# Last projections of a two-block network: turning activations inside the next projection, norm factor applied at eviction

## The reference, cut to what matters

```python
y_hg = o_hg @ w_hg_out                                  # 1024 -> 2048
y_at = swa_sinks(qa, ka, va, sinks) @ w_at_out          # 1024 -> 2048
mixed = sigmoid(g_hg) * y_hg + sigmoid(g_at) * y_at
x = x + mixed @ w_out                                   # 2048 -> 2048
h2 = rmsnorm(x, norm_ffn)       # x * rsqrt(mean(x*x) + eps) * norm_ffn
x = x + square(relu(h2 @ w_up)) @ w_down                # 2048 -> 8192 -> 2048
```

## Time and profile before

| | us |
|---|---|
| median of 3 runs | 2844.6 |
| lowest and highest of them | 2839.79, 2845.03 |
| the profiled execution | 2837.94 |
| its span in the trace | 2836.0 |
| PE busy | 2599.0 (92%) |
| DVE busy | 1644.5 (58%) |
| ACT busy | 1307.8 (46%) |
| POOL busy | 346.7 (12%) |

### The profile page before, as it was taken

How to read it: one execution, slowest core, us unless ns; L and a number is a source line. 1 busy time by engine, 2 the same in 40 slices (tenths; PEclk the granted TensorE clock), 3 DMA queues, 4 the chain that set the end, 5 groups by cost and what they waited for, 6 DMA issues and landing times.

```text
span 2836.0 us, 35750 instructions
## 1 busy us (share of the span) xinstructions
PE 2599.0 (92%) x12310; PEld 2150.9 (76%) x12310; DVE 1644.5 (58%) x2435; ACT 1307.8 (46%) x1761; POOL 346.7 (12%) x242
## 2 busy tenths in 40 slices
PE   3579999999996899989789999999889999999999
PEld 2468877888885788768678778778668888888887
DVE  6877887777767644445575555544344444544543
ACT  2234444444434444434446666654444444444443
POOL 2200122111012000000000000005101111111111
PEclk9689999999998899999799999999989999999999
DMA  8878767878874634434345555535346655556553
GB/s 294 287 271 286 272 230 256 278 267 281 274 245 170 201 104 119 125 103 167 121 151 154 160 168 155 164 133 194 133 136 193 190 192 182 190 193 189 182 192 134
DMA packets 354931, 548.56 MB, mean 193 GB/s; under 512 B 31788, under 2 KB 117136, under 8 KB 354448
## 3 DMA queue, kind: packets, MB, share of 16 engines
q1 hardware_dynamic: 353152, 541.37, 57.6%
q10 hardware_dynamic: 1680, 5.91, 0.5%
HBM read 545.13 MB, written 2.10 MB: 193 GB/s over the span
## 4 chain that ended last, share of the span: by engine, by line
PE 62%; DVE 3%; ACT 2%; issue 1%; POOL 0%; ACTq 0%; DVEq 0%; POOLq 0%
PE ps L1256 18%; PE ps L1257 18%; PE ps L1258 18%; PE ps L1316 1%; PE ps L1253 1%; PE ps L1254 1%; PE ps L1255 1%; PE ps L1465 1%; PE ps L1466 1%; PE ps L1332 0%; DVE a_lo L750 0%; DVE tf L770 0%; ACT hi L370 0%; ACT a_hi L469 0%; DVE stage L1033 0%
## 5 line engine op out<-in xcount | busy, mean ns | idle before, releaser
L668 DVE TENSOR_TENSOR lo<-raw,hi 128x1024 fp32r<-128x1024 f32 x838 | 1046.5, 1262 | 869.2 <-ACT hi L370 867.8
L370 ACT ACTIVATE hi<-raw 128x1024 fp32r<-128x1024 f32 x838 | 879.0, 1058 | 834.2 <-PE ps L1258 804.6
L1256 PE MATMUL ps<-hi,a_hi 128*128 128x512 f32 (+2 forms) x2464 | 983.0, 399 | 43.8 <-DVE lo L668 29.4
L1257 PE MATMUL ps<-lo,a_hi 128*128 128x512 f32 (+2 forms) x2464 | 965.2, 392 | 0.0
L1258 PE MATMUL ps<-hi,a_lo 128*128 128x512 f32 (+2 forms) x2464 | 964.9, 392 | 0.0
L1256 PEld LDWEIGHTS ps<-hi,a_hi 128*128 128x128 f32 x2464 | 469.4, 190 | 153.3 <-issue 39.6
L1258 PEld LDWEIGHTS ps<-hi,a_lo 128*128 128x128 f32 x2464 | 468.9, 190 | 98.9
L1257 PEld LDWEIGHTS ps<-lo,a_hi 128*128 128x128 f32 x2464 | 469.7, 191 | 91.1
L1256 PE MATMUL ps<-hi,b_hi 128*128 128x512 f32 (+1 forms) x896 | 336.1, 375 | 1.4 <-DVE b_lo L746 1.4
L1257 PE MATMUL ps<-lo,b_hi 128*128 128x512 f32 (+1 forms) x896 | 334.9, 374 | 0.0
L1258 PE MATMUL ps<-hi,b_lo 128*128 128x512 f32 (+1 forms) x896 | 334.9, 374 | 0.0
(11 more groups left out here) (235 smaller groups left out, 1719.6 us busy)
## 6 DMA issues: line engine op xcount, KB each, us to landing
raw<-in_ada_w SPq DMA_DIRECT2D x96, 1024.0 KB
raw<-in_sgu_w_in SPq DMA_DIRECT2D x96, 1024.0 KB
raw<-in_w_up SPq DMA_DIRECT2D x64, 1024.0 KB
raw<-in_w_down SPq DMA_DIRECT2D x64, 1024.0 KB
raw<-in_w_in SPq DMA_DIRECT2D x42, 1024.0 KB
raw<-in_sgu_w_out SPq DMA_DIRECT2D x32, 1024.0 KB
raw<-in_w_in SPq DMA_DIRECT2D x128, 256.0 KB
raw<-in_mla_w_in SPq DMA_DIRECT2D x20, 1024.0 KB
```

The lines of the kernel that those rows point to most:

```text
L370: nc.scalar.activation(hi[:, q % CHUNKS, :], raw[:, r % RAWS, q % 2 * CW:(q % 2 + 1) * CW], ACT.Copy).then_inc(hi_ready, 1)
L668: nc.vector.tensor_tensor(lo[:, q % CHUNKS, :], raw[:, r % RAWS, q % 2 * CW:(q % 2 + 1) * CW], hi[:, q % CHUNKS, :].bitcast(F32), ALU.subt ...
L1256: mm(out_, x_hi, w_hi, start=start, stop=False)
L1257: mm(out_, x_hi, w_lo, start=False, stop=False)
```

## The change

Steps 2 to 6 above are rearranged.

- `w_hg_out` and `w_at_out` go by column block: block 0 of the one, block 0 of the other, block 1 of the one, and so on. The sum of a column block is thus ready after its `w_at_out` block. Its two groups are turned to A (`mixed`) behind the first and third chunk of the next `w_at_out` block. The groups of the last column block are turned behind the fourth and fifth chunk of the first `w_out` block.
- x is turned too, as it is, into B with the gain `norm_ffn` (`added`, `gained`): two groups behind the third and sixth chunk of the next `w_out` block, the last two behind the fourth and fifth chunk of the first `w_up` block. The squares of a column block (`act_block_squares`) stand behind the first group of the next block on ACT.
- The factor rstd is no longer multiplied into x. It is the scale of the relu eviction of `w_up` (`normed=True`), which waits for it (`n_rstd`). y is not written any more.
- `w_up` reads B in place of A, so the buffers swap their parts in the rest. The four blocks of `w_out` and the first four of `w_up` are written out, not looped.

PE around the second junction, before: the end of `w_out` and the start of the transposes (L1316); `n_out` counts y's rows, `t_lo` DVE's lo parts.

The diff, cut to its core (DVE's part follows ACT's group for group):

```diff
-            for m in ("w_hg_out_2", "w_at_out_2"):
-                for b in range(4):
+            for b in range(4):
+                for m in ("w_hg_out_2", "w_at_out_2"):
                     sp_block(sp, n, d[m][0], b * NB, slabs=2)
...
+        def act_block_squares(act, n, src, b):
+
+            act.wait_ge(stage_free, 2 + n.stg.base)
+            for t in range(T):
+                act.wait_ge(block_sq, n.bsq.at(1))
+                nc.scalar.activation(block_junk[:, t * NB:(t + 1) * NB], src[:, t, b * NB:(b + 1) * NB], ACT.Square,
+                                     accum_out=bss[:, t, b:b + 1]).then_inc(block_sq, 1)
+                n.bsq.base += 1
...
         # act_result(..., normed=False)
+            if normed:
+                act.wait_ge(n_rstd, n.nrm.base)
...
-                nc.scalar.activation(to, ps[:, 2 * s + t, 0:width], func).then_inc(acc_free, 1)
+                nc.scalar.activation(to, ps[:, 2 * s + t, 0:width], func, scale=rstd[:, t:t + 1] if normed else 1.0).then_inc(acc_free, 1)
...
         # POOL
             for b in range(4):
-                c = slice(b * NB, (b + 1) * NB)
+                c, e = slice(b * NB, (b + 1) * NB), slice(D + b * NB, D + (b + 1) * NB)
                 pool_take(pool, n, lambda t: tt(v[:, t, c], v[:, t, c], stage[:, t, :], ALU.mult))
-            for b in range(4):
-                c, e = slice(b * NB, (b + 1) * NB), slice(D + b * NB, D + (b + 1) * NB)
                 pool_take(pool, n, lambda t: tt(v[:, t, e], v[:, t, e], stage[:, t, :], ALU.mult))
...
+        def pe_group(pe, n, src, g, sem, count):
+
+            pe.wait_ge(sem, count)
+            pe.wait_ge(t_lo, n.tg.base - 1)
+            for e in range(2):
+                for t in range(T):
+                    ins = nc.tensor.transpose(ps[:, 4 + n.tg.base % 2, e * S + t * P:e * S + (t + 1) * P], src(t, 2 * g + e), ident)
+            ins.then_inc(t_turned, 1)
+            n.tg.base += 1
...
-            for b in range(8):
-                pe_block(pe, n, B, kts=8, k0=8 * (b // 4))
-            pe.wait_ge(y_ready, 16)
-            pe_turn(pe, n, 8, cols(v))
-            pe_pairs(pe, n, A, 2)
-            pe.wait_ge(n_out, 8)
-            pe_turn(pe, n, 8, cols(y))
...
+            mixed = lambda g: pe_group(pe, n, cols(v), g, y_ready, 8 + 2 * (g // 2 + 1))
+            added = lambda g: pe_group(pe, n, cols(x), g, stage_free, 2 + BEFORE_FFN - 8 + 2 * (g // 2 + 1))
+            for b in range(4):
+                pe_block(pe, n, B, kts=8)
+                pe_block(pe, n, B, kts=8, k0=8, extra={0: lambda: mixed(2 * b - 2), 2: lambda: mixed(2 * b - 1)} if b else None)
+            for b in range(4):
+                if b:
+                    extra = {2: lambda: added(2 * b - 2), 5: lambda: added(2 * b - 1)}
+                else:
+                    extra = {3: lambda: mixed(6), 4: lambda: mixed(7), 5: lambda: pe.wait_ge(t_lo, n.tg.base)}
+                pe_block(pe, n, A, extra=extra)
+            for b in range(4):
+                pe_block(pe, n, B, extra=None if b else
+                         {0: lambda: pe.wait_ge(t_lo, n.tg.base), 3: lambda: added(6), 4: lambda: added(7),
+                          5: lambda: pe.wait_ge(t_lo, n.tg.base)})
...
-                pe_blocks_turning(pe, n, A, ffn(c), before + ready)
+                pe_blocks_turning(pe, n, B, ffn(c), BEFORE_FFN + ready)
```

More of the change, by code:

```diff
@@ L109 @@
 STAGED = 2 * 60
+BEFORE_FFN = STAGED - 8 * 8
 def raw_of(chunk):
@@ L377, in act_steps, with act_result @@
                 n.chunk.base += 1
-        def act_result(act, n, dst, func=ACT.Copy, aset=None, width=NB):
+        def act_result(act, n, dst, func=ACT.Copy, aset=None, width=NB, normed=False):
             act.wait_ge(chunk_used, n.chunk.at(CHUNKS))
+            if normed:
+                act.wait_ge(n_rstd, n.nrm.base)
             for t in range(T):
@@ L406, in act_pairs, with act_blocks_turning @@
                     act_result(act, n, (lambda t: dst(i, b, t)) if dst else None, func)
-        def act_blocks_turning(act, n, dst_hi, func, dst=None):
+        def act_blocks_turning(act, n, dst_hi, func, dst=None, normed=False):
             for b in range(4):
@@ L415, in act_blocks_turning @@
                 act_steps(act, n, 2)
-                act_result(act, n, (lambda t: dst(b, t)) if dst else None, func)
+                act_result(act, n, (lambda t: dst(b, t)) if dst else None, func, normed=normed)
+        def act_block_squares(act, n, src, b):
[5 more added lines that the diff above has]
+                n.bsq.base += 1
         def act_pairs_squared(act, n, dst, src, raws=8):
@@ L643, in _ @@
             act_split(act, n, 4, b_hi[:, 8:16, :])
-            for b in range(8):
+            mixed = lambda g: act_split(act, n, 1, a_hi[:, 2 * g:2 * g + 2, :], fresh=True)
+            gained = lambda g: act_split(act, n, 1, b_hi[:, 2 * g:2 * g + 2, :], fresh=True,
+                                         scale=lambda k: va[:, A_FFN + 2 * g + k:A_FFN + 2 * g + k + 1])
+            for b in range(4):
                 act_steps(act, n, 4)
                 act_result(act, n, None)
-            act_split(act, n, 8, a_hi)
@@ L648, in _ @@
-            act_pairs_squared(act, n, None, x)
-            act_root(act, n)
-            act_split(act, n, 8, a_hi, scale=lambda k: va[:, A_FFN + k:A_FFN + k + 1])
-            act_pairs(act, n, 2, None, ACT.Relu)
+                if b:
+                    act_steps(act, n, 1)
+                    mixed(2 * b - 2)
+                    act_steps(act, n, 2)
+                    mixed(2 * b - 1)
+                    act_steps(act, n, 1)
+                else:
+                    act_steps(act, n, 4)
@@ new lines, in _ @@
+                act_result(act, n, None)
+            for b in range(4):
+                if b:
+                    act_steps(act, n, 3)
+                    gained(2 * b - 2)
+                    act_block_squares(act, n, x, b - 1)
+                    act_steps(act, n, 3)
+                    gained(2 * b - 1)
+                    act_steps(act, n, 2)
+                else:
+                    act_steps(act, n, 4)
+                    mixed(6)
+                    act_steps(act, n, 1)
+                    mixed(7)
+                    act_steps(act, n, 3)
+                act_result(act, n, None)
@@ L652, in _ @@
+            act_steps(act, n, 4)
+            gained(6)
+            act_steps(act, n, 1)
+            gained(7)
+            act_block_squares(act, n, x, 3)
+            act_root(act, n)
+            act_steps(act, n, 3)
+            act_result(act, n, None, ACT.Relu, normed=True)
+            for b in range(3):
+                act_steps(act, n, 8)
+                act_result(act, n, None, ACT.Relu, normed=True)
             for c in range(3):
-                act_blocks_turning(act, n, b_hi, ACT.Relu)
+                act_blocks_turning(act, n, a_hi, ACT.Relu, normed=True)
@@ L654, in _ @@
                 if c < 2:
                     act_pairs(act, n, 2, None)
-            act_blocks_turning(act, n, a_hi, ACT.Copy)
+            act_blocks_turning(act, n, b_hi, ACT.Copy)
             for b in range(4):
@@ L788, in dve_pairs, with norm_x @@
                     ada_keep(dve, n, ada[0], i * 4 + ada[1])
[L790 to L795, removed]
+        def norm_x(dve, n):
+            dve_norm(dve, n, D)
             for t in range(T):
@@ L1113, in _ @@
             dve_split(dve, n, 4, b_hi[:, 8:16, :], b_lo[:, 8:16, :])
[L1114 to L1119, removed]
+            mixed = lambda g: dve_split(dve, n, 1, a_hi[:, 2 * g:2 * g + 2, :], a_lo[:, 2 * g:2 * g + 2, :])
+            gained = lambda g: dve_split(dve, n, 1, b_hi[:, 2 * g:2 * g + 2, :], b_lo[:, 2 * g:2 * g + 2, :],
+                                         scale=lambda k: va[:, A_FFN + 2 * g + k:A_FFN + 2 * g + k + 1])
+            for b in range(4):
+                if b:
+                    dve_steps(dve, n, 5)
+                    mixed(2 * b - 2)
+                    dve_steps(dve, n, 2)
+                    mixed(2 * b - 1)
+                    dve_steps(dve, n, 1)
+                else:
+                    dve_steps(dve, n, 8)
+            for b in range(4):
+                if b:
+                    dve_steps(dve, n, 3)
+                    gained(2 * b - 2)
+                    dve_steps(dve, n, 3)
+                    gained(2 * b - 1)
+                    dve_steps(dve, n, 2)
+                else:
+                    dve_steps(dve, n, 4)
+                    mixed(6)
+                    dve_steps(dve, n, 1)
+                    mixed(7)
+                    dve_steps(dve, n, 3)
+            dve_steps(dve, n, 4)
+            gained(6)
+            dve_steps(dve, n, 1)
+            gained(7)
+            blocks_norm(dve, n)
+            dve_steps(dve, n, 3)
+            dve_steps(dve, n, 24)
             for c in range(3):
-                dve_blocks_turning(dve, n, b_hi, b_lo)
+                dve_blocks_turning(dve, n, a_hi, a_lo)
```

(2 more changed lines are left out.)

14 lines of the change are left out of this document (8 added, 6 removed).

## The result

| | before | changed |
|---|---|---|
| median of 4 runs each | 2843.11 | 2802.98 |
| lowest to highest | 2839.79 to 2845.03 | 2801.44 to 2809.11 |
| profiled execution | 2837.94 | 2801.44 |
| its span | 2836.0 | 2799.6 |

The ratio of the times is 0.9863, with a 95% interval of 0.9848 to 0.9877: 1.4% faster. The forecast was 2809 us in a range of 2800 to 2820, from a gain of 35.3 us. The medians give 40.1 us, the two spans 36.4 us.

The account below looks back on a forecast made before the run. PE was taken to set the pace; removing both junctions' holes and low clock (43.24 us) less 7.92 us for 16 groups gives 35.3 us, so 2844.6 - 35.3 = 2809.3, say 2809 us, range 2800 to 2820.

Parts of the forecast that it names:

- The bound: From the junctions on, PE sets the pace; a hole taken out of PE comes off the time.
- The sum: Both junctions: holes 16.49 and 21.93 us plus low clock 1.77 and 3.05 removed, 7.92 back for transposes; net 35.3 us.
- The group price of 0.495 us: Each of 16 groups turned between matmuls costs PE 0.495 us, from `w_up` turning blocks' 22.75 us; 7.92 us together.
- The weak term: Matmuls behind the two junctions run at granted clocks 0.81 and 0.59, losing 1.77 and 3.05 us, which the change removes.
- The covers: Each group turned in the stream gets its data and gives its result in time; margins 0.7 to over 4 us.
- The margin on POOL: Last column block's mixed groups, first `w_out` block: POOL's sums end 1.5 us before PE's group needs them.
- The one on ACT: First `w_up` block: squares (2.18 us), root and rounding leave chunk 8's lo part ready 1.1 us before PE.
- B: Some groups come late at the last column blocks, 1 to 4 us each; gain 27 to 34 us; chance 0.15.
- C: Each group in the stream lowers the clock, 3.05 us each, 48.8 us lost, 13.5 us slower; chance 0.02.
- D: Loads lived on the two pauses, so holes reappear as waits for slabs; gain near 0; chance 0.02.
- The rule of the Trainium skill: DVE and POOL lock each other out per instruction: POOL's sums take 11.2 us, PE wants them at 10.9; gain 35.0.
- The step from the profiled execution to the median: Whole kernel: median of the runs before lies 6.7 us above the profiled execution; forecast 2844.6 - 35.3 = 2809.3 us.

Follow-up runs that it names:

- e1: Kernel before with only the first junction dissolved (mixers' projections by column block, mixed groups turned in the stream); ratio to before 0.994, stretch 935.2 us against 951.9.
- e2: Kernel before with only the second junction dissolved (x turned inside `w_out` and first `w_up` block, rstd at relu eviction); ratio to before 0.9924, stretch 928.0 us.
- e4: Changed kernel with the four transposes of each of the 16 new groups done twice; ratio to before 0.9895, stretch 923.0 us against 916.6.
- e3: Kernel before with rstd at the relu eviction, no y, x turned in a row behind the last `w_out` block; ratio to before 0.9986, stretch 945.7 us.
- e5: Changed kernel with the last two mixed groups two chunks earlier in the first `w_out` block; one run, 2807.6 us, stretch 918.4 us.
- e6: Changed kernel with two unread copies on ACT between last squares and root in the first `w_up` block; one run, 2812.5 us, stretch 917.3 us.
- e8: Changed kernel with the attention's four groups turned behind the chunks of the first `w_hg_out` block; ratio to before 0.9861, stretch 908.4 us.

## Why the prediction was right

**The bound.** PE sets the pace in this part, and holes of PE come off the time in full: shown by e1 and e2, whose stretches close to within 0.2 us when hole, clock, groups and the kind of the mark are added up.

**The sum.** 43.24 less 7.92 is 35.3 us, and the stretches differ by 35.3. The holes, 16.49 and 21.93, were right in every kernel that keeps them (16.1 to 16.5, 21.8). The group price of 0.495 us, taken from the pitch of other blocks, was right; its split into transposes and break is 0.40 and 0.10 by e4, where that expectation had taken 0.35 and 0.145.

**The weak term** was the clock. 1.77 and 3.05 us were read from one execution; behind the first hole, unchanged, e3 loses 1.7 and e2 nothing, and behind the second, unchanged, e1 loses 1.7. The prediction also read the 1.77 us as a clock that stayed down behind the hole; it had come back in the hole and fell anew. The sum met the trace to a tenth because it was set against the very execution that those numbers came from, and because the changed kernel's execution had the same kind of mark: so close a match is luck. By these samples the term lies between 1.7 and 4.8 us for both junctions, and the working should have carried both ends. The gain would then have been 32 to 35 us, within the stated range.

**The covers** all held. The margin on POOL was 1.7 us (forecast 1.5). The one on ACT was 2.1 (forecast 1.1): the step that was mis-sized is the squares, whose 2.18 us contained a wait for POOL. e5 and e6 show that both margins are real and worth one for one when used up, less 1.1 us by which POOL became faster in e5.

**The rivals.** B, late groups, did not happen; e5 shows what it would have looked like. C, the clock falling at groups in the stream, is refuted by e4, with twice the transposes and no low clock. D, the loads, is refuted by 205 us at 180 GB/s without a hole. The rule of the Trainium skill (SBUF — State Buffer, "SBUF: two separate sides"), taken at its worst, would have cost PE 0.3 us; the trace shows no wait of PE there.

**The median.** 2802.98 is 6 us below the forecast. The step from the profiled execution to the median took the 6.7 us between them as fixed. Nothing fixes them: the part ahead of the mark varies by 9.4 us between two executions of one and the same kernel. Where the 6 us lie in these very runs can't be shown, since only one of them has a trace. That the median fell inside the range rests on a range wide enough for this spread, and not on the step.

## What to carry to other kernels

A junction at which all activations are turned in a row is worth its whole length, less some 0.5 us a group here, if its groups can be turned one by one while other matmuls run: put each group behind a chunk of matmuls, one chunk ahead of its first use, and check three distances in the trace, data ready, result ready, and what else stands in the queue of the engine that copies it. A per-row norm factor that can be moved behind the projection is worth little by itself (6 of 21.9 us here); it matters because it takes the norm out of the way of the turning. Compare traces from a common mark at the point of the change, since the part ahead of it can move by several us; here it moved by 9.4, more than e3 or e8 won.

## What the runs showed of the hardware

- The clock behind a hole is no fixed price. Behind some 16 us without long matmuls, with transposes in them, 512-column steps lost 1.7 us twice, 2.4 once and nothing once; behind 22 us they lost 3.0 and 1.7. Waits of 2.7 and 1.6 us lost nothing. In the hole of the first junction the granted clock came back to 1.00 while PE did nothing but transposes.
- GpSimd's two sums took 2.48 us beside an idle VectorE, 4.44 beside a busy one and 3.34 where VectorE ran dry half-way. The wait on GpSimd in e5 thus shortened itself by 1.1 us once it had stopped the others.
- The same instructions at the same place ran at a granted clock of 1.00 in five executions, 0.95 in three and 0.97 in two, over 200 us of short matmuls with pauses. Between the changed kernel's two traces that is 9 to 10 us of the whole, more than e3 or e8 won. What decides between them stays open.
